# Doing the last two weight panels ahead of a norm token half by token half

## The reference, cut to what matters

```python
# first model, for l in range(2)
x = _layernorm(DEEPNORM_ALPHA * x + merged @ w_out[l], ln1_g[l], ln1_b[l])
f = jnp.square(jax.nn.relu(x @ mlp_w1[l])) @ mlp_w2[l]
x = _layernorm(DEEPNORM_ALPHA * x + f, ln2_g[l], ln2_b[l])
# second model, for l in range(2)
u = _rmsnorm(h, norm_mix_g[l])
...
h = h + merged @ w_out[l]
u = _rmsnorm(h, norm_ffn_g[l])
...
h = h + (p[l] @ w_ple[l]) * jax.nn.sigmoid(h @ w_ple_gate[l])
return _rmsnorm(h, final_norm_g)
```

## Time and profile before

| what | value |
|---|---|
| time, median of 3 runs | 2624.01 us (2621.17 to 2626.75) |
| profiled execution: its time, its span | 2625.02 us, 2623.2 us |
| mean granted TensorE clock | 0.982 |
| PE busy (matmuls) | 2481.1 us, 95% of the span |
| DVE busy | 1796.4 us, 68% |
| ACT busy | 1442.4 us, 55% |
| POOL busy | 249.5 us, 10% |
| DMA, mean | 162 GB/s |
| chain that ended last, by engine | PE 76%, DVE 13%, ACT 5%, issue 3% |

### The profile page before, as it was taken

How to read it: one execution, slowest core, us unless ns; L and a number is a source line. 1 busy time by engine, 2 the same in 40 slices (tenths; PEclk the granted TensorE clock), 3 DMA queues, 4 the chain that set the end, 5 groups by cost and what they waited for, 6 DMA issues and landing times.

```text
span 2623.2 us, 42231 instructions
## 1 busy us (share of the span) xinstructions
PE 2481.1 (95%) x17296; PEld 2270.7 (87%) x17296; DVE 1796.4 (68%) x2928; ACT 1442.4 (55%) x2101; POOL 249.5 (10%) x193
## 2 busy tenths in 40 slices
PE   7999999999999999899999979999899999989998
PEld 7878988988889889799999778998898898778986
DVE  4567666556576665587778777884697668776874
ACT  4646644545465444476556635654666556535654
POOL 0000000000000000001114610000011207400000
PEclk9999999999999999999999999999999999989999
DMA  7444455555434556554457635665454467535663
GB/s 231 149 138 121 145 175 179 177 172 169 139 111 147 172 182 201 157 153 130 124 179 201 185 101 170 190 204 188 133 145 129 144 187 209 157 108 172 195 201 129
DMA packets 358958, 426.24 MB, mean 162 GB/s; under 512 B 21208, under 2 KB 286894, under 8 KB 358766
## 3 DMA queue, kind: packets, MB, share of 16 engines
q1 hardware_dynamic: 342890, 401.95, 49.1%
q10 hardware_dynamic: 14068, 15.91, 2.5%
q0 software_dynamic: 1808, 5.69, 0.8%
HBM read 422.35 MB, written 1.15 MB: 161 GB/s over the span
## 4 chain that ended last, share of the span: by engine, by line
PE 76%; DVE 13%; ACT 5%; issue 3%; DMA 1%; POOL 1%; SPq 1%; ACTq 0%; DVEq 0%
PE ps L112 75%; DVE wlo L121 3%; PE ps L115 2%; ACT L118 1%; POOL sE L124 1%; DVE sE L121 1%; ACT whi L118 1%; DVE xN L121 1%; ACT hgKm L118 1%; SPq L154 1%; DVE sz L130 0%; DVE sx L124 0%; ACT rms L118 0%; ACT E L118 0%; DMA memN<-in_mem 0%
## 5 line engine op out<-in xcount | busy, mean ns | idle before, releaser
L121 DVE TENSOR_TENSOR wlo<-wring,whi 128x1024 fp32r<-128x1024 f32 x768 | 918.2, 1218 | 232.2 <-ACT whi L118 232.0
L118 ACT ACTIVATE whi<-wring 128x1024 fp32r<-128x1024 f32 x768 | 802.4, 1054 | 464.7 <-PE ps L112 454.7
L112 PE MATMUL ps<-uT,whi 128*128 128x256 f32 x4640 | 827.5, 283 | 21.9 <-DVE wlo L121 9.3
L112 PEld LDWEIGHTS ps<-uT,whi 128*128 128x128 f32 x4640 | 712.1, 190 | 33.3 <-issue 19.9
L112 PE MATMUL ps<-uT,wlo 128*128 128x256 f32 x2320 | 648.8, 280 | 0.0
L112 PEld LDWEIGHTS ps<-uT,wlo 128*128 128x128 f32 x2320 | 441.0, 190 | 0.0
L112 PE MATMUL ps<-xT,whi 128*128 128x256 f32 x2112 | 387.1, 287 | 14.3 <-DVE wlo L121 11.1
L112 PEld LDWEIGHTS ps<-xT,whi 128*128 128x128 f32 x2112 | 329.0, 192 | 22.0 <-DVE wlo L121 12.5
L112 PE MATMUL ps<-xT,wlo 128*128 128x256 f32 x1056 | 298.6, 283 | 0.0
L112 PE MATMUL ps<-whi,hid 128*128 128x512 f32 x864 | 268.5, 390 | 1.6 <-DVE wlo L121 1.6
L112 PEld LDWEIGHTS ps<-xT,wlo 128*128 128x128 f32 x1056 | 202.9, 192 | 0.1
(11 more groups left out here) (377 smaller groups left out, 3553.0 us busy)
## 6 DMA issues: line engine op xcount, KB each, us to landing
wring<-in_w_in SPq DMA_DIRECT2D x346, 512.0 KB, 4.3
wring<-in_mlp_w SPq DMA_DIRECT2D x128, 512.0 KB, 4.3
wring<-in_w_up SPq DMA_DIRECT2D x88, 512.0 KB, 4.6
wring<-in_w_down SPq DMA_DIRECT2D x44, 512.0 KB, 4.5
wring<-in_w_branch SPq DMA_DIRECT2D x32, 512.0 KB, 3.3
wring<-in_w_out SPq DMA_DIRECT2D x32, 512.0 KB, 3.9
wring<-in_mem_w_kv SPq DMA_DIRECT2D x16, 512.0 KB, 5.3
wring<-in_w_br_hg SPq DMA_DIRECT2D x16, 512.0 KB, 4.7
```

The costliest lines, as they stand in the source:

```text
L112: return self.e.matmul(*p, **k) if self.e else Nothing()
L118: return self.e.activation(*p, **k) if self.e else Nothing()
L121: return self.e.tensor_tensor(*p, **k) if self.e else Nothing()
```

## The change

`projA` gets an argument `early`. In the last block of 512 columns of such a stage, the last two panels are done in this order: both panels for half 0, then `out(0, ...)`, then both panels for half 1, then `out(1, ...)`. The last panel is marked `late`: the splits that used to stand behind its `panel` step (high part of the panel three further, low part of the panel two further) now stand behind its matmuls for half 1. The steps of the statistics take a half: `ln_stats`, `ln_last`, `sum_part`, `rms_rate` (POOL's power, on its own), `rms_scale` and `final_rows` follow each half's `out`. For the last layernorm with the RMS norm behind it the steps of half 1 are written out. The final gain row is loaded by a step of its own ahead of the gate stage, behind the same panel as before. `early` is set for `w_out` (both blocks), `mlp_w2` (both), `w_out_2` (both) and `w_ple_gate_2` (both): eight stages.

```diff
+    def projA(w, c0, n, x, out, r0=0, k0_=0, banks=None, first=True, fin=True, early=False):
+
 
         chunks = x.n // 512
         for b0 in range(0, n, 512):
+            pair = []
             nb = min(512, n - b0)
             step = min(chunks, WN // nb)
             us = [PB.take() for _ in range(2)] if banks is None else banks[b0]
             for k0 in range(0, chunks, step):
                 nk = min(step, chunks - k0)
                 p = panel([(0, w[r0 + k0 * 128:r0 + (k0 + nk) * 128, c0 + b0:c0 + b0 + nb])], nk, nb)
-                do("tokens", p, x, us, k0_ + k0, first and k0 == 0, fin and k0 + nk == chunks)
+                q = (p, x, us, k0_ + k0, first and k0 == 0, fin and k0 + nk == chunks)
+                if early and b0 + nb == n and k0 + 2 * step >= chunks:
+                    pair.append(q)
+                    do("tokens", *q, (0,))
+                    if len(pair) == 2:
+                        p.late = True
+                        us[0].full = ("panel", p.i, 0)
+                        out(0, b0, nb, us[0])
+                        for q in pair:
+                            do("tokens", *q, (1,))
+                else:
+                    do("tokens", *q, (0, 1))
                 for t in range(2):
                     us[t].full = ("panel", p.i, t)
                 yield
             if out is not None:
-                for t in range(2):
+                for t in range(1 if pair else 0, 2):
...
+        def out_r(x, n, ready, done):
+            def out(t, b0, nb, u):
+                do("residual", x, n, t, b0, u, ready(t))
+                if b0:
+                    done(t)
+            return out
         gb = gain_rows(l, "ln1_g", "ln1_b", ("ln1", l))
         n = ln_open(l, rN, "ln1_g", "ln1_b", ("ln1", l))
-        run(projA(a["w_out"][l], 0, 1024, merged, out_r(xN, n, lambda t: [("rows", ("ln2", l - 1), t)] if l else ["x"])))
-        do("ln_stats", n)
+        run(projA(a["w_out"][l], 0, 1024, merged, out_r(xN, n, lambda t: [("rows", ("ln2", l - 1), t)] if l else ["x"], lambda t: do("ln_stats", n, t)), early=True))
...
+                    xN2 = ar.take("xN", 2048, at=34368)
+                    done = lambda t: do("ln_stats", n, t)
+                    if l == DEPTH - 1:
+                        norm = rms_open(("mix", 0), None, 34304, n.res.again(), xN2)
+
+                        def done(t):
+                            if t:
+                                do("square_rows", norm, 0, [("rows", n.tag, 0)])
+                                do("rms_rate", norm, 0)
+                            do("ln_last", n, gb, xN2, t)
+                            if t:
+                                do("rms_scale", norm, 0)
+                                do("square_rows", norm, 1, [("rows", n.tag, 1)])
+                                do("rms_rate", norm, 1)
+                                do("rms_scale", norm, 1)
+                    out = out_r(xN1, n, lambda t: [("rows", ("ln1", l), t)], done)
+                run(projA(w2, 0, 1024, hid, out, (q - 1) * 1024, banks=banks, first=q == 1, fin=q == 4, early=q == 4))
...
     def after(t, b0, tag, n):
         if n:
             do("square_part", n, t, b0 // 512, (tag, t, b0 // 512))
-        if t:
-            if n:
-                do("sum_part", n, b0 // 512)
+            do("sum_part", n, b0 // 512, t)
             if b0:
-                hkey[0], hkey[1] = ([(tag, i, 0), (tag, i, 1)] for i in range(2))
+                do("rms_rate", n, t)
+                do("final_rows" if n.tag == "final" else "rms_scale", n, t)
+        if t and b0:
+            hkey[0], hkey[1] = ([(tag, i, 0), (tag, i, 1)] for i in range(2))
 
     def rms_turn(n, l, g, x):
 
-        do("rms_scale", n)
         turned_by_halves(n.u3, lambda c, t: [("rms", n.tag, t, c // 4)], to_pair_scaled(x, g, l))
...
+        run(projA(a["w_out_2"][l], 0, 1024, merged, add_to_h(("h1", l), norm), early=True))
...
+            norm.gain = ar.take("gain", 1024, at=0)
+            do("load_final_gain", norm)
...
+        run(projA(a["w_ple_gate_2"][l], 0, 1024, hT, out_g, early=True))
...
-        if kind == "panel":
+        if kind == "panel" and not args[0].late or kind == "tokens" and args[0].late and args[-1] == (1,):
...
+    def tokens(p, x, us, q0, first, fin, halves):
         e.wait_ge(*at(("lo", p.i)))
-        for t in range(2):
+        for t in halves:
...
+    def ln_stats(n, t):
         r3 = n.res.tok()
-        for t in range(2):
-            e.wait_ge(*at(("lnscale", n.tag, t)))
-            e.scalar_tensor_tensor(out=n.nm[:, t:t + 1], in0=n.mv[:, t, 0:1], scalar=-1.0, in1=n.rs[:, t:t + 1], op0=ALU.mult, op1=ALU.mult).then_inc(
-                *up("dve_ln", ("lnshift", n.tag, t)))
-            if t == 0:
-                e.wait_ge(*now("dve_ln"))
-                for h in range(2):
-                    v = r3[:, 0, h * 512:h * 512 + 512]
-                    e.tensor_scalar(v, v, n.rs[:, 0:1], n.nm[:, 0:1], ALU.mult, ALU.add).then_inc(*up("dve_ln", ("ln", n.tag, 0, h)))
...
+    def sum_part(n, h, t):
+        e.wait_ge(*at(("rmssum", n.tag, t, h)))
...
+    def rms_scale(n, t):
+
+        if t:
+            return
...
+    def final_rows(f, t):
         e.wait_ge(*at("fingain"))
-        for t in range(2):
-            e.wait_ge(*at(("rmsscale", f.tag, t)))
-            for h in range(2):
-                v = slice(h * 512, h * 512 + 512)
...
+    def ln_stats(n, t):
+        e.wait_ge(*at(("lnvar", n.tag, t)))
+        power(n.rs[:, t:t + 1], n.tmp[:, t:t + 1], ("lnscale", n.tag, t))
+
+    def ln_last(n, gb, out, t):
+        ln_stats(n, t)
+
+    def rms_rate(n, t):
+        e.wait_ge(*at(("rmsvar", n.tag, t)))
+        power(n.rs[:, t:t + 1], n.tmp[:, t:t + 1], ("rmsscale", n.tag, t))
```

More of the change, by code:

```diff
@@ L792, in block1 @@
         if l == DEPTH - 1:
-            xN2 = ar.take("xN", 2048, at=34368)
-            do("ln_last", n, gb, xN2)
             ar.give(gb)
-            return xN2, None, n.res.again()
-        do("ln_stats", n)
-        xT2, xN2 = ar.pair("xT", 8), ar.take("xN", 2048, at=34368)
+            return xN2, None, norm
+        xT2 = ar.pair("xT", 8)
         ln_features(n, xT2)
@@ L822, in schedule @@
     hkey = [[("rows", ("ln2", DEPTH - 1), t)] for t in range(2)]
-    norm = rms_open(("mix", 0), None, 34304, later)
-    for t in range(2):
-        do("square_rows", norm, t, hkey[t])
+    norm = later
     def add_to_h(tag, n=None):
@@ L1223, in schedule @@
         norm = block2(l, norm)
-    f = K.fin = norm
-    f.gain = ar.take("gain", 1024, at=0)
-    do("final_norm", f)
     K.steps, K.panels = [], panels
@@ L2157, in ln_last @@
-    def ln_last(n, gb, out):
+        e.wait_ge(*at(("lnscale", n.tag, t)))
+        e.scalar_tensor_tensor(out=n.nm[:, t:t + 1], in0=n.mv[:, t, 0:1], scalar=-1.0, in1=n.rs[:, t:t + 1], op0=ALU.mult, op1=ALU.mult).then_inc(
+            *up("dve_ln", ("lnshift", n.tag, t)))
+        if t == 0:
+            e.wait_ge(*now("dve_ln"))
+            for h in range(2):
+                v = r3[:, 0, h * 512:h * 512 + 512]
+                e.tensor_scalar(v, v, n.rs[:, 0:1], n.nm[:, 0:1], ALU.mult, ALU.add).then_inc(*up("dve_ln", ("ln", n.tag, 0, h)))
@@ L2159, in ln_last @@
+    def ln_last(n, gb, out, t):
         for i in range(2):
             e.wait_ge(*at(("gb", n.tag, i)))
-        for t in range(2):
-            o = out.tok()[:, t, :]
-            e.scalar_tensor_tensor(out=o, in0=n.res.tok()[:, t, :], scalar=n.mv[:, t, 0:1], in1=gb.ap[:, 0:1024], op0=ALU.subtract, op1=ALU.mult).then_inc(
-                *up("dve_rows"))
-            e.wait_ge(*now("dve_rows"))
-            e.wait_ge(*at(("lnscale", n.tag, t)))
-            e.scalar_tensor_tensor(out=o, in0=o, scalar=n.rs[:, t:t + 1], in1=gb.ap[:, 1024:2048], op0=ALU.mult, op1=ALU.add).then_inc(
-                *up("dve_rows", ("rows", n.tag, t)))
+        o = out.tok()[:, t, :]
+        e.scalar_tensor_tensor(out=o, in0=n.res.tok()[:, t, :], scalar=n.mv[:, t, 0:1], in1=gb.ap[:, 0:1024], op0=ALU.subtract, op1=ALU.mult).then_inc(
+            *up("dve_rows"))
+        e.wait_ge(*now("dve_rows"))
+        e.wait_ge(*at(("lnscale", n.tag, t)))
+        e.scalar_tensor_tensor(out=o, in0=o, scalar=n.rs[:, t:t + 1], in1=gb.ap[:, 1024:2048], op0=ALU.mult, op1=ALU.add).then_inc(
+            *up("dve_rows", ("rows", n.tag, t)))
@@ L2530, in ple_gate @@
         e.tensor_tensor(v, v, pv, ALU.add).then_inc(*up("dve_resid", (tag, t, b0 // 512)))
[L2532 removed]
+    def final_rows(f, t):
         e.wait_ge(*at("fingain"))
[L2534 to L2539 removed]
+        e.wait_ge(*at(("rmsscale", f.tag, t)))
+        for h in range(2):
+            v = slice(h * 512, h * 512 + 512)
+            e.scalar_tensor_tensor(out=f.u3[:, t, v], in0=f.h[:, t, v], scalar=f.rs[:, t:t + 1], in1=f.gain.ap[:, v], op0=ALU.mult, op1=ALU.mult).then_inc(
+                *up("dve_rows", ("final", t, h)))
```

(30 more changed lines are left out.)

52 lines of the change are left out of this document (19 added, 33 removed).

## The result

The kernel after takes 2644.09 us (median of 4 runs, 2639.89 to 2649.48) where the kernel before takes 2623.22: a ratio of 1.0079, 95% interval 1.0057 to 1.0102. It is slower, as forecast, but by 20.7 us where 13.4 were predicted, and 2.1 above the predicted range.

The account below looks back on a forecast made before the run. PE is busy nearly the whole span, so time changes only where PE stands still. Chains gave +7.0 us and the clock +6.4, +13.4 in all: 2637.4 us on the median of 2624.0, range 2627 to 2642.

Parts of the forecast that it names:

- Order on DVE: DVE's queue: half 1's residual waits behind half 0's scaling and a split of about 1.2 us; 1.7 late at site 1.
- sites 1 to 3: Layernorms near 378, 570 and 890 us: half 1's chain +1.3 us each; the clock is lost there either way.
- Sites 5 and 7: RMS norms after w_out_2, at 1630 and 2396 us: half 1's chain +1.5 us each, bounds 1.3 and 1.8.
- +2.0 for 5 and 7: Clock falls behind these two RMS norms, after a 3.5 us wait between the halves' transposes: +2.0 us each.
- site 6: RMS norm after the gate, 1848 us: chain about 0, bounds -0.5 and +0.8; clock +1.2 us.
- site 4: Last layernorm with an RMS norm behind it, 1079 us: chain +0.3 us, clock +1.2 us.
- The order of the matmuls at nothing: Last two panels of each changed stage: reordering adds no matmuls and makes no split late, priced at nothing.
- site 8: Final norm, 2614 us: no panel follows, so no split in the way; -0.2 us, bounds -0.5 and +0.3.
- B: Rival: chains as reckoned but the clock no worse anywhere; 2631 us, chance 0.25.
- C: Rival: half 0's early transposes keep the clock up at sites 1 to 3, winning 6.6 us; 2624 us, chance 0.10.
- D: Rival: half 1 meets an idle DVE and half 0's transposes are time won; 2615 us, chance 0.08.
- E: Rival: everything in the forecast at its upper bound; 2643 us, chance 0.07.

Follow-up runs that it names:

- lo_back: Kernel after, with the low-part split of the panel two further back behind the last panel's `panel` step, ahead of half 0's residual: 2639.0 us, ratio 1.0047.
- fc_early: Kernel after, with the step that transposes and copies the convolution's columns moved inside the w_out_2 stage, behind its second block's first panel: 2639.5 us, ratio 1.0050.
- after_busy: Kernel after, with 24 more identity transposes on PE between the halves at sites 1 to 3: 2639.9 us, ratio 1.0053.
- before_busy: Kernel before, with 18 more identity transposes on PE ahead of half 0's transposes at sites 1 to 3: 2624.0 us, ratio 0.9990.
- lo_fc: Kernel after, with the edits of both lo_back and fc_early: 2638.0 us, ratio 1.0040.
- after_dense: Kernel after, with extra 128x512 matmuls, results never read, in PE's waits at the halved stages: 2633.5 us, ratio 1.0024.
- order_only: Kernel before, with only the new order of the last two panels' matmuls: 2627.2 us, ratio 1.0005.
- before_dense: Kernel before, with extra 128x512 matmuls in PE's wait ahead of transposes at every stage ending in a norm: 2623.9 us, ratio 0.9988.
- mixed_dense: Like lo_fc, but layernorms at sites 1 to 3 scaled wholly on ACT, sites 5 and 7 whole, dense matmuls in waits: 2621.0 us, 0.9979 of kernel before.

## Why the prediction was right and wrong

**Order on DVE: right.** The split in front of residual 1 was called the term that decides among the chains. DVE's order, residual 1 at 2.10 behind the last matmul (2.1 predicted), ACT at 4.81 (4.82 worked out) and the wait of 3.91 (3.8) came as written, and `lo_back` took the split's 1.1 to 1.3 away. The stretches grew 1.3 to 1.5 at sites 1 to 3; at site 1 the excess over 1.3 is half 1's transposes, which ran at 1.2 GHz in 1.97 instead of 1.82.

**"Sites 5 and 7 ... +1.5 each": wrong, +3.1.** The chain itself was right in its order and a little high: in `fc_early`, where only that is left, ACT scales half 1 3.84 behind the last matmul, 2.54 before, +1.3, the lower bound. That the stretch there grew by 1.55 and so met the 1.5 is in part luck: half 1's 8 transposes now ran at 1.2 GHz (1.97). What I missed is that the moved step `rms_scale` passes another one on ACT. The prediction went through DVE's, SP's and POOL's queues and stopped on ACT at its split. On ACT the copies `fc<-ps` fell behind half 1's scaling, 4 of half 0's transposes need the banks that they free, and half 1's 8 stand behind those 4. The prediction put this wait at nothing; it cost 1.6 a site. A bank is a wait as good as a datum, and the earlier trace rows could not show it since it was met early.

**"Sites 1 to 3 lose it either way", and +2.0 for 5 and 7: wrong in size.** They lose it either way, 7.98 instead of 6.16 in the profiles; but `fc_early` lost 5.5 there with the same steps at these sites, so that the loss grew at sites 1 to 3 is not shown. Sites 5 and 7 lost 2.94 and 2.80, site 6 1.68 (1.2 taken), site 4 nothing (1.2 taken). At 4 and 6 one profile decides nothing: site 4, with the same steps, lost 1.9 in `after_busy` and 2.3 in `before_busy`, whose site 4 is that of the kernel before. In sum 9.2 where 6.4 stood, and 11.2 by the runs with the clock held, which hold the slower transposes too. The argument for sites 5 and 7 was also only half right: it named a wait of 3.5, but `lo_fc` lost as much with one of 2.21. In the Trainium skill, "TensorE: Matmul & The Clock Gate", section "Part 1: The HAM clock gate", the slow clock is the default and activity releases it. `after_dense` agrees (1.00 at site 1 with PE kept at work through the wait); in `after_busy`, with 24 more transposes in the wait and 1.29 and 1.53 us of it left, the clock was 0.50 behind the restart.

**Site 4: right in kind, +0.6 for +0.3.** POOL's powers beside DVE's row operations, kernel after, beside the earlier trace rows:

```profile
1086.04 1.56 POOL L121 TENSOR_TENSOR lnst<-lnst,cst 128x1 f32<-128x1 f32 x1 [19.61 <-DVE lnst L124]
1092.04 1.52 POOL L121 TENSOR_TENSOR rmss<-rmss,cst 128x1 f32<-128x1 f32 x1 [4.43 <-DVE rmss L124]
1093.53 0.54 POOL L121 TENSOR_TENSOR lnst<-lnst,cst 128x1 f32<-128x1 f32 x1
```

Twice the slow value beside a row operation (DVE's started at 1085.89 and 1091.88), and 0.54 with DVE idle. The same holds in all fourteen profiles: the 24 powers that began beside this row operation took 1.52 to 1.56, the 180 that began with DVE idle 0.54 to 0.57, and the 12 beside a residual, which has one operand in PSUM, 0.56 to 0.57. These rows agree with the rule cited from the Trainium skill, "SBUF — State Buffer", section "SBUF: two separate sides"; no run here took the row operation away. What made +0.6 of +0.3 is that ACT's scaling came 1.1 later (1.0 reckoned) and the transposes of half 0 gave back 0.6 instead of 0.8.

**The order of the matmuls at nothing, site 6 at about 0 and site 8 at -0.2: right** (`order_only` 1.0005, +0.2, -0.3).

**What 13.4 lacked.** The sites came to 20.2 us. Of the 6.8 more, 3.2 are the banks at sites 5 and 7, 2.8 the clock's loss, and 0.8 small excesses of the chains. The prediction also had no term for the slower pace of one stage, 4.4 us of the profiled pair; the last section has it.

**The rivals.** B (clock no worse) fell with the windows at site 5 and with `after_dense`; C (clock kept at 1 to 3) with the windows of site 1; D with residual 1 at 2.10 and the wait of 3.91. E, everything at its upper bound, gave 2643 and had 0.07: nearest to the measured time, but the banks at sites 5 and 7 are not among its bounds, so it would have been near by luck. Its stated bounds, with site 4 at the +0.3 that has no upper bound, sum to 18.1, or 2642, the end of the range, and not to 2643.

## What to carry to other kernels

When a step moves in an in-order list, walk every engine's list past it, and for each step that it passes ask which data, and which banks, are waited for behind it. Before splitting a wait in two to hide half of it, check which half sets the restart: here it was the other one, and starting the hidden half earlier gave nothing. Count the clock as a term of its own: here a stage's pause cost up to 2.9 us in slow matmuls behind it, about as much as the largest change of the pause itself (3.1). Unused dense matmuls in the wait, 19 at a layernorm site of `after_dense`, took that loss away; for the whole kernel they gave 14.4 us back in the halved order and 3.2 in the kernel before.

## What the runs showed of the hardware that was not expected

**Two paces at full clock.** The feed-forward stage's matmuls of 256 columns ran at either of two paces with no wait and a granted clock of 1.00. Kernel after, the same 85 us stretch of layer 0 and layer 1:

```profile
1655.00:1740.00 85.00, 85.00 (x753) 85.00 (x752) 70.83 (x108) 56.42 (x79) 0.00 (x0) 1.00 0.59 183
```

```profile
2425.00:2510.00 85.00, 85.00 (x724) 85.00 (x723) 67.08 (x103) 54.06 (x76) 0.00 (x0) 1.00 0.58 180
```

753 matmuls against 724. The kernel before had 753 and 752 in these two windows. The pace holds for all 1056 of these matmuls, some 120 us: from the last matmul ahead of site 5 to the one ahead of site 6 `before_dense` took 218.1 us, and `mixed_dense`, which had 724 in both layers and the same stretch of 5.69, took 222.7. These some 4.5 us are the rest of the profiled difference of 24.5. In the profiled `mixed_dense`, which took 2628.8 and was the slowest of its 12 executions, they came twice; which pace its fastest, 2613.2, had is not known. The slower pace came in 5 of the 28 stages profiled, with code that had the other pace elsewhere; its cause is open. Every median here may hold some of it, which is one more reason not to read differences of a few us.

**The clock's loss differs between executions.** Site 5 has the same code in `after` and `after_busy`; it lost 2.94 in one profile and 0.00 in the other. So one profile's loss at one site says little; the counts over many sites, the mean clocks and the medians are what the argument rests on.
